# Layer 2 of a decoder trunk: query projection, attentions and output projection as one instruction stream

## The reference, cut to what matters

```python
u = rmsnorm(h, mix_norm[1])
proj = u @ fox_w_in[0]                         # 1024 -> 768 + 256
q_fox, q_mem = proj[..., :768], proj[..., 768:]
logits = (q_t . k_s) / sqrt(128) + c[t] - c[s]   # for s <= t, blocks of 128 queries
main = softmax(logits) @ v                     # per head
mem = softmax(q_mem . k_mem / 8) @ v_mem       # 4 heads of 64, 256 memory tokens
h = h + [main | mem] @ w_out[1]                # 1024 -> 1024
```

## Time and profile before

| | us |
|---|---|
| median of 3 runs | 2201.84 (2195.1 to 2201.98) |
| profiled execution | 2193.12 |
| its span, first to last instruction | 2191.3 |

### The profile page before, as it was taken

How to read it: one execution, slowest core, us unless ns; L and a number is a source line. 1 busy time by engine, 2 the same in 40 slices (tenths; PEclk the granted TensorE clock), 3 DMA queues, 4 the chain that set the end, 5 groups by cost and what they waited for, 6 DMA issues and landing times.

```text
span 2191.3 us, 25400 instructions
## 1 busy us (share of the span) xinstructions
PE 2112.5 (96%) x9944; PEld 1734.6 (79%) x9944; DVE 933.4 (43%) x865; ACT 819.3 (37%) x923; POOL 440.2 (20%) x287
## 2 busy tenths in 40 slices
PE   7999999989989999999999999999999899999998
PEld 6888888867668978888888888888886478888886
DVE  6543333566444235333343443333334645333323
ACT  4422222377433344343322244442222535444221
POOL 3312210312143422212111012121110112212211
PEclk9999999999999999999999999999998999999999
DMA  5243323322100113333233433332333013333232
GB/s 170 86 130 96 90 87 98 100 77 77 39 1 1 39 40 96 96 96 96 84 94 100 154 116 96 96 96 77 95 120 131 1 39 96 96 96 96 79 98 73
DMA packets 319227, 188.71 MB, mean 86 GB/s; under 512 B 10537, under 2 KB 316858, under 8 KB 318906
## 3 DMA queue, kind: packets, MB, share of 16 engines
q1 hardware_dynamic: 317472, 180.38, 28.4%
q10 hardware_dynamic: 826, 4.27, 0.5%
q0 software_dynamic: 864, 3.15, 0.3%
HBM read 182.53 MB, written 5.24 MB: 86 GB/s over the span
## 4 chain that ended last, share of the span: by engine, by line
PE 61%; DVE 1%; ACT 1%; issue 0%; ACTq 0%; POOL 0%; DVEq 0%; POOLq 0%
PE ps L471 19%; PE ps L473 19%; PE ps L472 19%; PE ps L883 1%; PE ps L529 0%; PE ps L864 0%; PE ps L555 0%; DVE f_stat L1745 0%; DVE fp L1741 0%; PE ps L852 0%; PE ps L546 0%; PE ps L873 0%; DVE w_lo L1286 0%; ACT bias_ts L1247 0%; ACT fp L1257 0%
## 5 line engine op out<-in xcount | busy, mean ns | idle before, releaser
L471 PE MATMUL ps<-x_hi,w_hi 128*128 128x512 f32 x1920 | 755.5, 393 | 16.4 <-DVE x_lo L1292 5.3
L473 PE MATMUL ps<-x_hi,w_lo 128*128 128x512 f32 x1920 | 749.7, 390 | 0.0
L472 PE MATMUL ps<-x_lo,w_hi 128*128 128x512 f32 x1920 | 749.6, 390 | 0.0
L914 ACT ACTIVATE w_hi<-raw 128x2048 fp32r<-128x2048 f32 (+1 forms) x188 | 324.3, 1725 | 787.7 <-PE ps L473 758.7
L1286 DVE TENSOR_TENSOR w_lo<-raw,w_hi 128x2048 fp32r<-128x2048 f32 (+1 forms) x188 | 412.6, 2195 | 221.3 <-ACT w_hi L914 221.0
L471 PEld LDWEIGHTS ps<-x_hi,w_hi 128*128 128x128 f32 x1920 | 362.3, 189 | 100.1 <-issue 13.6
L472 PEld LDWEIGHTS ps<-x_lo,w_hi 128*128 128x128 f32 x1920 | 362.0, 189 | 76.0 <-issue 1.7
L473 PEld LDWEIGHTS ps<-x_hi,w_lo 128*128 128x128 f32 x1920 | 361.9, 188 | 75.9
L473 PE MATMUL ps<-hid_hi,w_lo 128*128 128x512 f32 x704 | 273.9, 389 | 0.0
L471 PE MATMUL ps<-hid_hi,w_hi 128*128 128x512 f32 x704 | 273.9, 389 | 0.0
L472 PE MATMUL ps<-hid_lo,w_hi 128*128 128x512 f32 x704 | 273.9, 389 | 0.0
(11 more groups left out here) (271 smaller groups left out, 1623.9 us busy)
## 6 DMA issues: line engine op xcount, KB each, us to landing
raw<-in_ffn_w_gate_up SPq DMA_DIRECT2D x176, 512.0 KB, 5.0
raw<-in_ffn_w_down SPq DMA_DIRECT2D x64, 384.0 KB, 3.7
raw<-in_ffn_w_down SPq DMA_DIRECT2D x64, 320.0 KB, 3.0
raw<-in_gdn_w_in SPq DMA_DIRECT2D x26, 512.0 KB, 4.7
raw<-in_w_out SPq DMA_DIRECT2D x16, 512.0 KB, 4.4
raw<-in_kv_w SPq DMA_DIRECT2D x12, 512.0 KB, 4.6
raw<-in_mem_w_kv SPq DMA_DIRECT2D x8, 512.0 KB, 4.1
raw<-in_fox_w_in SPq DMA_DIRECT2D x8, 512.0 KB, 4.0
```

The source lines that it names most:

```text
L471: nc.tensor.matmul(dst, hi, xh, start=first, stop=False)
L472: nc.tensor.matmul(dst, hi, xl, start=False, stop=False)
L473: return nc.tensor.matmul(dst, lo, xh, start=False, stop=last)
L914: nc.scalar.activation(w_hi[s][:, 0:n], raw[s][:, 0:n], ACT.Copy).then_inc(hi_ready, 1)
```

## The change

The phase `fox0` is gone. Its work is laid into `foxin0` and `wout1`:
- The query projection is written out per column tile. The first unit is as before. In units 1 to 3 there are 16 places each, one after every three matmuls; `beside` puts other work there: the turn of c, the six turns of values (unit 1), and forgetting attention steps 0 to 3 (unit 1), 4 to 19 (unit 2), 20 to 27 (unit 3), where 24 to 27 only finish the earlier ones; then the scores of the first two memory heads. A head's blocks go from the longest to the shortest. Results go out tile by tile (`tile_done`, `tile_evac`), the queries scaled by 1/sqrt(128) at once.
- The weights of units 2 and 3 of this stream are rounded and cut in halves between steps.
- c goes to DRAM in the `kv0` phase (GpSimd's queue). At the end of `down2` ScalarE issues three DMAs: values, keys, and c to all 128 partitions (`c_b`, 6 x 512 each). GpSimd masks the diagonal block in `c_b` itself, before each step and after the step before it has used it. VectorE adds score and column of c and subtracts `c_b`. The product that spread c and ScalarE's bias are gone.
- ScalarE copies the turned values. A head's result is rounded by ScalarE straight from PSUM to `fox_hi`, and VectorE makes `fox_lo` from PSUM.
- In `wout1` the first two output units take head results as they come, with the rest of the memory attention (a pair of heads at a time, the two heads' products alternating) between their columns. The feeding of `x_hi` and `x_lo` for the next FFN starts with the first unit.

The core of the diff, each part with 8 columns of indentation less:

```diff
+FOX_STEPS = HEADS * TT
+FOX_START = {1: (12, 0), 2: (0, 4), 3: (2, 20)}
+VALUES_BESIDE = (2, 4, 6, 8, 10, 12)
+COLUMNS_BESIDE = 5
+MEM_SCORES_BESIDE = 12
...
+def fox_block(n):
+    return n // TT, TT - 1 - n % TT
...
-fq_mem = fox.put("fq_mem", [P, MT, SEQ])
 fv = fox.put("fv", [P, TT, WIDTH])
...
+            pe.wait_ge(lo_ready, u + 1)
+            pe.wait_ge(tile_evac, 3)
+            for hd in range(2):
+                pe.wait_ge(mix_ready, KT + hd + 1)
+                column(0, hd, 0, first=hd == 0)
+            pe.wait_ge(evac, g)
+            for hd in range(2):
+                column(0, hd, 1, first=hd == 0)
+            for hd in range(2, HEADS):
+                pe.wait_ge(mix_ready, KT + hd + 1)
+                for o in range(2):
+                    column(0, hd, o)
+                if hd == 3:
+                    mem_turn(0, 0)
+                if hd == 4:
+                    mem_turn(0, 1)
+            pe.wait_ge(lo_ready, u + 2)
+            for hd in range(2):
+                column(1, hd, 0, first=hd == 0)
+            mem_values(0)
+            mem_scores(1)
+            for hd in range(2, HEADS):
+                column(1, hd, 0)
+            pe.wait_ge(mix_ready, KT + HEADS + 1)
+            for o in range(2):
+                column(0, HEADS, o)
+            column(1, HEADS, 0)
+            mem_turn(1, 0)
+            column(1, 0, 1, first=True)
+            mem_turn(1, 1)
+            column(1, 1, 1)
+            mem_values(1)
+            column(1, 2, 1)
+            column(1, 3, 1)
+            pe.wait_ge(mix_ready, KT + HEADS + 2)
+            column(0, HEADS + 1, 0, last=True)
+            column(0, HEADS + 1, 1, last=True).then_inc(unit_done, 1)
+            column(1, HEADS + 1, 0, last=True)
+            for c in (4, 5, 6):
+                column(1, c, 1)
+            column(1, HEADS + 1, 1, last=True).then_inc(unit_done, 1)
+            for n in (2, 3):
+                pe.wait_ge(lo_ready, u + n + 1)
+                bank_free(g + n)
+                for c in range(KT):
+                    for o in range(2):
...
+            def fox_step(n):
+                if n < FOX_STEPS:
+                    hd, i = fox_block(n)
+                    if n == 0:
+                        pe.wait_ge(k_back, 16)
+                        pe.wait_ge(evac, g + 1)
+                        pe.wait_ge(c_cols_ready, 1)
+                    if n % TT == 0 and hd >= 2:
+                        if hd % 2 == 0:
+                            pe.wait_ge(tile_evac, hd // 2)
...
                                                    fp[m % FOX_DEEP][:, s * P:(s + 1) * P], ident[:])
                     last.then_inc(f_turned, 1)
...
-                    hd, i = divmod(m, TT)
+                    hd, i = fox_block(m)
+                    if m % TT == 0:
+                        if hd == 0:
+                            pe.wait_ge(tile_evac, 1)
+                        elif hd == 1:
+                            pe.wait_ge(evac, g + 2)
+                        else:
+                            pe.wait_ge(mix_ready, KT + hd - 1)
                     pe.wait_ge(f_copied, m + 1)
...
+            def mem_scores(t):
+                if t == 0:
+                    pe.wait_ge(tile_evac, 3)
...
+                for i in range(TT):
+                    for e in range(2):
+                        r0 = MEM_HEAD * e
+                        last = nc.tensor.matmul(
+                            ps[:, 4 + 2 * e + i // 2, (i % 2) * MEM_LEN:(i % 2 + 1) * MEM_LEN],
+                            fq_mem[r0:r0 + MEM_HEAD, t, i * P:(i + 1) * P],
+                            mem_k[r0:r0 + MEM_HEAD, 1, t, :], start=True, stop=True)
+                        if i == TT - 1:
+                            last.then_inc(ma_score, 1)
...
+            def beside(n, s):
+                if n == 1 and s == COLUMNS_BESIDE:
+                    turn_columns()
+                if n == 1 and s in VALUES_BESIDE:
+                    turn_values(VALUES_BESIDE.index(s))
+                after, first = FOX_START[n]
+                m = first + s - after
+                if s >= after and m < FOX_STEPS + 4:
+                    fox_step(m)
+                if n == 3 and s == MEM_SCORES_BESIDE:
+                    mem_scores(0)
+            unit(u, g, x_hi, x_lo, feed=KT * feeds_before[fed_by[name]])
+            spread_sum(fed_by[name])
+            for n in range(1, 4):
+                s, bank = slot(u + n), (b0, b1, b0, b0)[n]
+                pe.wait_ge(lo_ready, u + n + 1)
+                for o in range(2):
+                    if n == 1:
+                        pe.wait_ge(evac, g)
+                    elif n == 2:
+                        pe.wait_ge(evac, g + 1)
+                    elif o == 0:
+                        pe.wait_ge(tile_evac, 2)
+                    else:
+                        pe.wait_ge(evac, g + 3)
+                    for c in range(KT):
+                        at = c * 2 * P + o * P
+                        last = split_products(ps[:, bank + o, :], w_hi[s][:, at:at + P],
+                                              w_lo[s][:, at:at + P], x_hi[:, c, :], x_lo[:, c, :],
+                                              c == 0, c == KT - 1)
+                        if c == KT - 1:
+                            last.then_inc((tile_done, unit_done)[o], 1)
+                        beside(n, KT * o + c)
...
+            if name == "down2":
+                for b in range(2):
+                    act.wait_ge(kv_spilled[b], 16 * (HEADS // 2))
+                act.wait_ge(c_spilled, 16)
+                act.dma_start(fvt[:], kv_spill[:, HEADS:2 * HEADS, :]).then_inc(v_back, 16)
+                act.dma_start(fk[:], kv_spill[:, 0:HEADS, :]).then_inc(k_back, 16)
+                act.dma_start(c_b[:], c_spill.rearrange("(o h) t -> o h t", o=1).broadcast_to(
+                    [P, HEADS, SEQ])).then_inc(c_back, 16)
...
+                                     ACT.Copy).then_inc(mix_hi, 1)
+            exponentials(0, 0)
+            exponentials(0, 1)
+            round_hi(u + 1)
+            copy_turned(0, 0)
+            copy_turned(0, 1)
+            memory_hi(0)
+            exponentials(1, 0)
+            exponentials(1, 1)
+            copy_turned(1, 0)
+            copy_turned(1, 1)
+            memory_hi(1)
+            round_hi(u + 2)
...
+                act.wait_ge(evac, g + n + 1)
+                for c in (2 * n, 2 * n + 1):
+                    feed_hi(x_hi[:, c, :], h[:, c, :], gains[:, gain + c:gain + c + 1])
+                if n:
+                    round_hi(u + n + 2)
...
+            for n in range(FOX_STEPS + 5):
+                if n < FOX_STEPS:
+                    hd, i = fox_block(n)
                     act.wait_ge(f_max, n + 1)
                     nc.scalar.activation(fp[n % FOX_DEEP][:, 0:(i + 1) * P], fp[n % FOX_DEEP][:, 0:(i + 1) * P],
                                          ACT.Exp, bias=f_stat[:, n % FOX_DEEP, 0:1],
                                          accum_out=f_stat[:, n % FOX_DEEP, 1:2]).then_inc(f_exp, 1)
...
+                if 3 <= n < FOX_STEPS + 3:
                     m = n - 3
-                    i = m % TT
+                    hd, i = fox_block(m)
                     act.wait_ge(f_turned, m + 1)
                     if m >= 2:
                         act.wait_ge(f_pv, m - 1)
                     nc.scalar.activation(fpt[m % 2][:, 0:(i + 1) * P], ps[:, 6 + m % 2, 0:(i + 1) * P],
                                          ACT.Copy).then_inc(f_copied, 1)
+                if n in (6, 7):
+                    round_hi_part(u + 3, n - 6)
+                if n in (22, 23):
+                    round_hi_part(u + 4, n - 22)
+                if n >= 8 and n % TT == 0:
+                    hd = n // TT - 2
+                    act.wait_ge(f_pv, TT * (hd + 1))
+                    nc.scalar.activation(fox_hi[:, hd, :], ps[:, b1 + hd % 2, :], ACT.Copy).then_inc(mix_hi, 1)
...
+            negative_max(0, 0)
+            negative_max(0, 1)
+            dve.wait_ge(unit_done, u)
+            nc.vector.tensor_tensor(fq_mem[:, 1, :], ps[:, bank_of(g) + 1, :], rstd[:],
+                                    ALU.mult).then_inc(evac, 1)
+            normalise(0, 0)
+            normalise(0, 1)
+            cut_lo(u + 1)
+            memory_lo(0)
+            negative_max(1, 0)
+            negative_max(1, 1)
+            normalise(1, 0)
+            normalise(1, 1)
+            memory_lo(1)
...
+                nc.vector.tensor_tensor(hs, ps[:, b0:b0 + 2, :], hs, ALU.add).then_inc(evac, 1)
+                if n == 0:
+                    cut_lo(u + 2)
+                for c in (2 * n, 2 * n + 1):
+                    feed_lo(name, x_lo[:, c, :], h[:, c, :], gains[:, gain + c:gain + c + 1],
+                            x_hi[:, c, :], c)
+                if n:
+                    cut_lo(u + n + 2)
...
+            for n in range(FOX_STEPS + 6):
+                if n < FOX_STEPS:
+                    hd, i = fox_block(n)
```

(43 more changed lines are left out.)

327 lines of the change are left out of this document (187 added, 140 removed).

## The result

The changed kernel takes 2161.76 us (median of 4 runs, 2160.3 to 2163.31), the kernel before 2201.34 us beside it (median of 4, 2195.1 to 2201.98). The ratio is 0.9827, 95% interval 0.9807 to 0.9846: 39.6 us less. The forecast was 2165.3 us, from a gain of 36.5.

What follows compares the result with a forecast made beforehand. It took TensorE, busy 96% of the span, as the bound, with layer 2's middle latency-bound: 139.4 + 7.8 + 2.7 = 149.9 us in place of 186.37, 36.5 less, giving 2165.3 us; range 2156 to 2184 us.

Steps and rivals of the forecast that it cites:

- the floor: TensorE's work at full clock from layer 2's query projection through output projection: 87.0 + 4.0 + 32.7 + 15.7 = 139.4 us.
- the waits: TensorE's waiting added to its work in layer 2: 7.8 us in the stream, 2.7 in the output projection.
- The 4.0 beside the units: TensorE's work beside the eight projection units: sum of squares 0.85, turn of c 0.54, 24 value turns 2.6 us.
- rival C: Memory products run in pairs: scores fall 5.4 to 3.4, value products 6.8 to 3.4; gain 45, 2157 us; chance 0.13.
- The chain in a step: Forgetting attention: value products of n-4 wait for ScalarE's copy behind the exponential of n-1; 0.65 us a head, 3.9 for six.
- Weight cuts: VectorE's cuts at stream steps 8, 9 and 24, 25 make TensorE late: 1.4 us each, 2.8 for two.
- The start of the pipeline: Filling the forgetting attention's pipeline at its first step in the query projection: 0.5 us.
- The output projection: Waits there, with memory attention: bank, second pair's turns and value products, last split, unit 2's weights; sum 2.7 us.
- The front: Three DMAs on ScalarE's queue (values, keys, c: 4.7 MB) land in time: charged 0, up to 3 us.
- B: Chain in the stream as late as before, both engines' weight halves paid in full: gain 22, 2180 us; chance 0.18.
- D: Slower: c, a 12 KB source read 128 times, lands late, 121 us after wanted; 2286 us; chance 0.04.
- E: Stream does not overlap, a wait holding a projection unit until a head is through: gain 0 to 12 us; chance 0.05.

Runs made afterwards that it cites:

- the kernel with both orders first: Changed kernel with VectorE's scaling before its add, ScalarE's copy before its exponential, fourth query unit's cut in quarters, third output unit's weights in halves: 2151.91 us, ratio 0.9787.
- the kernel with those three edits: Changed kernel with VectorE's scaling before its add, fourth query unit's cut in quarters and third output unit's weights in halves: 2152.42 us, ratio 0.9788.
- the scaling first: Changed kernel with VectorE's reciprocal and scaling of block n-2 moved ahead of the add of block n: 2160.81 us, ratio 0.983.
- the halves: Changed kernel with the third output unit's weights rounded and cut in two halves: 146.17 us from first query product to next FFN, against 147.4.
- Later splits: Changed kernel with head results copied from PSUM by VectorE and all six split after the last step: 2162.12 us, ratio 0.9842.
- the kernel without the interleaving: Changed kernel with forgetting attention steps and first memory scores after the fourth query unit: 2175.5 us, ratio to before 0.9901.

## Why the prediction was right

The gain of the stretch was forecast as 36.5 us and is 38.9. Two sums were off in opposite directions, and that they partly cancel is luck: the floor was 4.6 us too high, the waits 2.1 too low.

**The floor.** Forecast 139.4, and 134.8 with the memory products as they ran. Projection and the six heads' products needed no correction: the kernel with both orders first runs the whole stretch in 3.8 us more than the sum. The 4.0 beside the units was small by 0.3; its own equation (45.89 = 4 x 10.88 + 0.85 + 0.54 + 0.88) is already 0.1 short. The memory products were mis-sized. 5.4 and 6.8 us were charged, 3.9 and 3.7 were taken. Two errors lie in that: the overlap was left out, and the drain was taken too large, 0.24 us off each group where the next product shows 0.07 (1739.82 to 1741.69 for a record of 1.94). With the right drain the charge would have been 13.2 instead of 12.2. The forecast had seen that 16 records in 2.94 us were less than twice 8 in 1.99, and gave rival C 0.13; its mechanism came true in full, its 45 us did not, since the waits did not shrink with it. The Trainium skill (TensorE: Matmul & The Clock Gate, Part 3) has small products in distinct row or column groups run concurrently; the trace agrees, with 2.00 us for 16 score records where 8 took 1.99, and 1.94 for eight value records in place of 1.93 for four. With one head's scores behind the other's it agrees only in part: 2.96. It was the row of 16 against 8 that should have tipped it: had nothing overlapped it would have been 3.7, so the only question was how much a closer order would add.

**The chain in a step.** Forecast 0.65 us a head, measured 1.1: the 384, 256 and 128 wide steps of the third head take 0.46, 0.13 and 0.46 us more than their products. The step that failed is "The value products of n-4 need ScalarE's copy of n-4". That is true and was reckoned rightly, but it was the only chain followed. The turn of n-3 hangs on VectorE's scaling of n-3, which stands in VectorE's order behind the maximum of n-1, and so behind the score of n-1. These rows of the changed kernel show it: the scaling of the 512 wide block (L2043) starts at 1693.86, when the maximum of the 256 wide block (L2022) is through, and the add before it had waited for its score (the row names the turn that stands right behind the score on TensorE).

```profile
1692.81 0.48 DVE L2018 SCALAR_TENSOR_TENSOR fp<-ps,c_cols,c_b 128x256 f32<-128x256 f32 x1 [0.26 <-PE ps L955]
1693.33 0.42 DVE L2022 TENSOR_REDUCE f_stat<-fp 128x1 f32<-128x256 f32 x1
1693.67 0.15 DVE L2041 RECIPROCAL f_stat<-f_stat 128x1 f32<-128x1 f32 x1
1693.86 0.49 DVE L2043 TENSOR_SCALAR fp<-fp,f_stat 128x512 f32<-128x512 f32 x1
```

Only when that was out of the way did the waits for the copy appear, 0.4, 0.2 and 0.13 us in a head of the kernel with those three edits: 0.73 in sum against the forecast's 0.65, though not step by step (0.2, 0.36 and 0.08).

**Weight cuts.** Forecast 1.4 each. The first cost 1.2 (steps of 3.20, 2.32 and 2.13 us where the third head has 2.66, 1.79 and 2.01) and the second about 1.0 (1717.65 to 1718.89, less a product of 0.23). The size of the first was about right and the reason half right, since not VectorE's load but the scaling queued behind the cut was what TensorE felt. The second has another origin, which the forecast did not have: VectorE stood idle for 1.69 us before that cut, until ScalarE had rounded both halves, and the scaling stood behind it.

```profile
1717.06 1.23 DVE L1502 TENSOR_TENSOR w_lo<-raw,w_hi 128x1024 fp32r<-128x1024 f32 x1 [1.69 <-ACT w_hi L1079]
```

**The start of the pipeline.** Forecast 0.5, measured 1.25 in the step at 1663.63 (the next begins at 1666.22), nearly all of it the same wait for the scaling. With the scaling first it is 0.4, but the step behind it then waits 0.7 for ScalarE's copy, until the copy is first too.

```profile
1665.83 0.63 PE L955 MATMUL ps<-ident,fp 128*128 128x128 f32 x4 [0.94 <-DVE fp L2043]
```

**The output projection.** Forecast 2.7 us. The wait for unit 2's weights was forecast as 1.1 and is 1.16 (1760.69, a product of 0.23, then 1762.08); the halves gave it back. The second value products waited 0.6, as forecast, the second pair's turns 0.1 and 0.2 instead of 0.3. The 0.45 for a bank and the 0.25 for the last split did not show; no start in their places is over 0.1 us late. The 1.5 us that the forecast gave the lower clock at the start of this stage are 1.7 by its own two numbers (45.24 and 43.5); they are no term of the sum.

**What was charged at nothing.** The front: values, keys and c landed 6.3, 9.6 and 13.4 us after their issue, and no turn, score or add waited for them. The masks on GpSimd: no wait of VectorE for them. Later splits: 0.2 us. The clock: 1.00.

**The rivals.** B (a chain as late as before, every cut in full) would have left a stretch of 164 us; it is refuted by 147.4, though the waits in a head were two thirds more than forecast. D is refuted by the landing of c. E would have shown a head outside the projection; the kernel without the interleaving shows what that costs, 13.3 us.

**The base.** "Nothing outside this part should move" holds for 1571 us to 0.2 us. Layer 1's mixing took 7.2 us more in the profiled execution, for no reason in the change. The forecast from the profiled execution, 2156.6, missed the profiled 2161.66 by 5.1 us; the median less the gain missed by 3.5. The gain itself was missed by 2.4 us; the rest lies in the base, which was 2.2 us above the median of all runs of the kernel before, and in the scatter of the changed kernel's runs.
